# Reordering the work inside an expert tile of a hybrid attention and mixture-of-experts layer: the shares of a result added behind their own down product, the fold ahead of the pick, and a copy of x1 in plain order

## The reference, cut to what matters

```
x1 = x + gt_m * rms_norm(y_mixer, g_post_mix)
h  = rms_norm(x1, g_pre_ffn) * (1 + sc_f) + sh_f
combine = top-1 group, then top-2 experts in it, with gates     # (tokens, 32)
for every expert e:
    a = h @ w1[e];  b = h @ w3[e]                               # "up", 2048 -> 512 twice
    hid = silu(a) * b * combine[:, e]
    y += hid @ w2[e]                                            # "down", 512 -> 2048
out = x1 + gt_f * rms_norm(y, g_post_ffn)
```

## Time and profile before

| | us |
|---|---|
| median of 3 runs | 1523.38 |
| lowest and highest run | 1520.29, 1523.55 |
| the profiled execution | 1522.02 |
| its span, from the first to the last instruction | 1520.2 |

### The profile page before, as it was taken

The page is one execution under the profiler, slowest core; times in us unless marked ns, Lnnn a source line. Parts: engine busy times, 40 slices in busy tenths (PEclk is TensorE's granted clock), DMA queues, the critical chain, the costliest instruction groups (busy, mean ns, idle before and its releaser), DMA issues.

```text
span 1520.2 us, 18000 instructions
## 1 busy us (share of the span) xinstructions
PE 1192.0 (78%) x7075; PEld 537.6 (35%) x7076; DVE 730.6 (48%) x977; ACT 178.1 (12%) x437; POOL 37.0 (2%) x66
## 2 busy tenths in 40 slices
PE   4799999999999998856756765775666579989755
PEld 4688544744444454212212211221221123333211
DVE  5776257777585635522432342243233226655526
ACT  3111132221111120000000000000000001110002
POOL 1001200000000001000000000000000000000000
PEclk9899999999999997978887887888788779999978
DMA  9999977898778778999999999999999999999995
GB/s 354 392 383 384 334 287 311 316 351 323 272 287 348 294 335 342 424 426 424 427 427 424 427 427 426 423 427 428 424 427 426 426 425 429 421 425 427 427 426 204
DMA packets 101636, 581.93 MB, mean 383 GB/s; under 512 B 6648, under 2 KB 31504, under 8 KB 57824
## 3 DMA queue, kind: packets, MB, share of 16 engines
q1 hardware_dynamic: 98000, 571.50, 92.2%
q10 hardware_dynamic: 2384, 7.77, 1.3%
q0 software_dynamic: 1216, 2.17, 0.5%
HBM read 579.29 MB, written 2.13 MB: 382 GB/s over the span
## 4 chain that ended last, share of the span: by engine, by line
PE 52%; DMA 34%; DVE 9%; SPq 2%; issue 1%; ACT 1%; POOL 0%; DVEq 0%; ACTq 0%
DMA stream<-in_w 32%; PE ps L848 12%; PE ps L674 11%; PE ps L759 7%; PE ps L874 6%; PE ps L593 5%; PE ps L804 3%; DMA stream<-in_w_ada 2%; PE ps L810 2%; PE ps L859 2%; SPq L463 2%; PE ps L671 1%; DVE cst L1276 1%; DVE wk L947 1%; DVE stream L1000 1%
## 5 line engine op out<-in xcount | busy, mean ns | idle before, releaser
L848 PE MATMUL ps<-stream,wk 128*32 128x512 f32 x2304 | 310.1, 699 | 251.3 <-DMA stream<-in_w 242.1
L1228 DVE TENSOR_TENSOR acc<-ps,acc 128x2048 f32<-128x2048 f32 x37 | 84.8, 2291 | 554.2 <-PE ps L810 554.2
L848 PEld LDWEIGHTS ps<-stream,wk 128*32 128x32 f32 x2304 | 87.2, 126 | 472.1 <-issue 470.0
L674 PE MATMUL ps<-stream 128*128 128x512 f32 x448 | 197.5, 594 | 0.3 <-PE ps L593 0.3
L874 PE MATMUL ps<-stream,cst 128*32 128x512 f32 x1152 | 131.1, 595 | 14.6 <-DVE cst L1280 14.6
L593 PE MATMUL ps<-stream 128*128 128x256 f32 x512 | 117.7, 393 | 2.2 <-ACT stream L1358 2.2
L674 PEld LDWEIGHTS ps<-stream 128*128 128x128 f32 x448 | 83.3, 190 | 99.2 <-issue 98.5
L759 PE MATMUL ps<-stream 128*128 128x512 f32 x256 | 112.3, 600 | 3.1 <-ACT stream L1462 1.8
L593 PEld LDWEIGHTS ps<-stream 128*128 128x128 f32 x512 | 100.8, 198 | 16.9 <-issue 2.2
L947 DVE SCALAR_TENSOR_TENSOR wk<-stream,cc,wk 128x768 f32<-128x768 f32 (+1 forms) x90 | 83.6, 929 | 11.1 <-DMA stream<-in_w_ada 8.5
L1501 ACT ACTIVATE wk<-ps 128x512 f32<-128x512 f32 x36 | 21.5, 597 | 549.9 <-PE ps L848 549.9
(11 more groups left out here) (258 smaller groups left out, 857.5 us busy)
## 6 DMA issues: line engine op xcount, KB each, us to landing
stream<-in_w SPq DMA_DIRECT2D x192, 2048.0 KB, 34.8
stream<-in_w_ada SPq DMA_DIRECT2D x64, 1024.0 KB, 5.5
stream<-in_w_in SPq DMA_DIRECT2D x8, 4096.0 KB, 16.6
stream<-in_w_ada SPq DMA_DIRECT2D x64, 384.0 KB, 10.0
stream<-in_w_out SPq DMA_DIRECT2D x4, 4096.0 KB, 15.4
stream<-in_w_ada SPq DMA_DIRECT2D x16, 512.0 KB, 9.4
stream<-in_w_in SPq DMA_DIRECT2D x4, 2048.0 KB, 14.3
stream<-in_w_in SPq DMA_DIRECT2D x2, 3072.0 KB, 16.2
```

What stands on the lines that cost most here:

```text
L674: last = nc.tensor.matmul(bank(fill % 2), hT[:, k, P * half:P * half + P], w[:, k, :], start=(k == 0), stop=(k == KD - 1))
L848: last = nc.tensor.matmul(bank(1)[32 * g:32 * g + 32, :], xe[:, k + g // 2, :], a13[g % 2][:, k + g // 2, :], start=(k == 0), stop=(k == K ...
L1228: V.tensor_tensor(y4, ps[:, b0:b0 + 4, :], y4, ALU.add).then_inc(ysum_sb, 1)
```

## The change

On PE a tile now adds the first share of its own result behind its down (with waits for ACT's copy of it, for the spread of this tile and for the earlier `collect`), so that the next tile has only the second share to add behind its up; the fold (L859) stands in front of `pick_rows()`, behind which the wait for `xp` follows at once. On DVE `collect(1, 4)` stands ahead of the chain of the gate, the copy to `xp` behind it, and `collect(0, 4)` at the end of the tile. The wait of the up for `spread` goes. Behind the loop the last tile's first share is already added. POOL, which has nothing to do in the loop, waits for the down of the last tile of expert 30, then copies x1 in plain order into the slot that this frees (`plain(t)`, two copies of 128x2048), and `residual(t)` reads it from there.

```diff
+        def plain(t):
+
+            return stream[:, 4, D * (t + 1):D * (t + 2)]
...
                 with pe.Fori(lo, hi) as t:
                     pe.wait_ge(xe_sb, t + 1)
-                    pe.wait_ge(spread_sb, t + 1)
...
                     pe.wait_ge(ye_sb, t + 1)
+                    pe.wait_ge(spread_sb, t + 1)
                     pe.wait_ge(ysum_sb, 2 * t + 2)
-                    add_part(0, 4)
-                    pe.wait_ge(pick_sb, t + 2)
-                    pick_rows()
+                    add_part(1, 4)
                     pe.wait_ge(ab_sb, t + 1)
                     for c in range(4):
                         last = nc.tensor.matmul(bank(1, 4, RT_W)[:, c, :], ...)
                     last.then_inc(h_ps, 1)
-                    pe.wait_ge(ysum_sb, 2 * t + 3)
-                    add_part(1, 4)
+                    pe.wait_ge(pick_sb, t + 2)
+                    pick_rows()
                     pe.wait_ge(rows_sb, t + 2)
                     pe.wait_ge(gated_sb, t + 1)
...
                     last.then_inc(ye_ps, 1)
+                    pe.wait_ge(spread_sb, t + 2)
+                    pe.wait_ge(ysum_sb, 2 * t + 3)
+                    pe.wait_ge(ye_sb, t + 2)
+                    add_part(0, 4)
...
-            pe.wait_ge(spread_sb, total + 1)
-            pe.wait_ge(ysum_sb, 2 * total + 2)
+            pe.wait_ge(xe_sb, total + 1)
+            pe.wait_ge(ysum_sb, 2 * total + 1)
...
-            earlier_sum(0)
-            pe.wait_ge(ye_sb, total + 1)
-            pe.nop(nofuse=True)
-            add_part(0, 4)
-            for g in range(1, 4):
+            for g in range(4):
                 earlier_sum(g)
             add_part(1, 0, True)
...
                 dve.wait_ge(part_ps, 2 * t + 1)
                 dve.wait_ge(ysum_sb, 2 * t + 2)
-                collect(0, 4)
-                dve.wait_ge(rows_ps, t + 2)
-                V.tensor_copy(xp, bank(0)).then_inc(rows_sb, 1)
-
+                collect(1, 4)
                 dve.wait_ge(h_exp, t + 1)
...
                 V.tensor_tensor(hid, hp[:, :, ROWS:2 * ROWS], eh, ALU.mult).then_inc(hid_sb, 1)
+                dve.wait_ge(rows_ps, t + 2)
+                V.tensor_copy(xp, bank(0)).then_inc(rows_sb, 1)
                 dve.wait_ge(xe_ps, t + 2)
...
                 dve.wait_ge(part_ps, 2 * t + 2)
-                collect(1, 4)
-
-            dve.wait_ge(part_ps, 2 * total + 1)
+                dve.wait_ge(ysum_sb, 2 * t + 3)
+                collect(0, 4)
+
             dve.wait_ge(ysum_sb, 2 * total + 2)
-            dve.nop(nofuse=True)
-            collect(0, 4)
-            dve.wait_ge(ysum_sb, 2 * total + 3)
...
+                dve.wait_ge(plain_sb, t + 1)
                 dve.wait_ge(fin_rs, t + 1)
...
-                    V.scalar_tensor_tensor(out=now, in0=now, scalar=st[:, 80 + t:81 + t], in1=by_model(t)[:, 32 * q:32 * q + 32, :],
+                    V.scalar_tensor_tensor(out=fin_gained(t)[:, c], in0=fin_gained(t)[:, c], scalar=st[:, 80 + t:81 + t], in1=plain(t)[:, c],
...
+            pool.wait_ge(route_sb, 1)
+            done = pool.value_load(cums[0:1, NE - 1:NE], min_val=1, max_val=MAX_TILES)
+            pool.wait_ge(ye_ps, done)
+            pool.nop(nofuse=True)
+            for t in range(TT):
+                nc.gpsimd.tensor_copy(plain(t).rearrange("p (q k) -> p q k", k=KD), by_model(t)).then_inc(plain_sb, 1)
```

More of the change, by code:

```diff
@@ L392, in build @@
             sem("hid_sb"), sem("ye_ps"), sem("ye_sb"))
-        gain_sb, fin_sq, fin_rs, fin_sb, fin_out = sem("gain_sb"), sem("fin_sq"), sem("fin_rs"), sem("fin_sb"), sem("fin_out")
+        plain_sb, gain_sb, fin_sq, fin_rs, fin_sb, fin_out = sem("plain_sb"), sem("gain_sb"), sem("fin_sq"), sem("fin_rs"), sem("fin_sb"), sem("fin_out")
         w_ada = a["w_ada"].rearrange("l (p k) (m n) -> (l p) k m n", p=P, m=6)
@@ L1295, in _ @@
             link(V.tensor_tensor(fin_gained(0), ysum[0], g2b, ALU.mult))
-            dve.wait_ge(part_ps, 2 * total + 2)
+            dve.wait_ge(part_ps, 2 * total + 1)
             dve.nop(nofuse=True)
@@ L1308, in residual @@
                     c = slice(512 * q, 512 * q + 512)
-                    now = fin_gained(t)[:, c].rearrange("p (q k) -> p q k", k=KD)
-                    V.scalar_tensor_tensor(out=now, in0=now, scalar=st[:, 80 + t:81 + t], in1=by_model(t)[:, 32 * q:32 * q + 32, :],
+                    V.scalar_tensor_tensor(out=fin_gained(t)[:, c], in0=fin_gained(t)[:, c], scalar=st[:, 80 + t:81 + t], in1=plain(t)[:, c],
                                            op0=ALU.mult, op1=ALU.add).then_inc(fin_sb, 1)
@@ L1509, in _ @@
             A(st[:, 83:84], cst[:, C_HALF:C_HALF + 1], ACT.Sqrt)
-            act.wait_ge(ysum_sb, 2 * total + 3)
+            act.wait_ge(ysum_sb, 2 * total + 2)
             act.nop(nofuse=True)
```

## The result

The changed kernel takes 1544.9 us (median of 4 runs, 1539.99 to 1545.02) against 1523.47: a ratio of 1.0136, with a 95% interval of 1.0122 to 1.0151. It is slower, as forecast, but by 21.4 us instead of 12, and outside the range. The profiled execution took 1544.78 us and spans 1542.9.

A forecast was written before the change was run, and what follows sets the result against it. From about 600 us the DMA engines' weight transfers were taken as the bound. Transfers +14.7 us and the end -2.7 gave +12.0, from the profiled 1522.02 to 1534.0, as median 1535.4 us; range 1528 to 1541.

The forecast's parts named there:

- where a longer tile is paid: From A's first up to E's second, weight transfers wait for PE; there a longer tile becomes a longer kernel, transfers +14.7 us.
- the two late issues: Weight transfers issued only when the second ups of B and E are done, at 1303.77 and 1391.08 us.
- the sum had 1.2: Slack at the issue behind E's second up: 1.2 us, taken off the 15.9 us by which that up ends later.
- the figure read from the row: Start and landing of transfers behind a late issue: 3.6 us, read from one transfer, against the skill's fixed cost of about 2.0.
- Loss 1: Ahead of the down, PE waits for DVE's copy to `xp`, now behind `hid`: down starts 0.62 us later.
- Loss 2: Behind the down, PE waits for ACT's copy to `ye`, then does `add_part(0, 4)`: +1.80 us a tile.
- The rival by which the wait for `xp` would not be on the path: Tile grows only about 1.0 us, 1524 us in all; needs PE to pass the `xp` wait; chance 0.04.
- The sum over the eight passages: From A's first up to E's second: 8 x 2.42 = 19.4 us, less 3.5 of vanishing waits, so 15.9 later.
- Queued behind this wait on PE is the next up: At the tile's end, the next up stands behind PE's wait for ACT's copy to `ye`; part of +1.80 us.
- a rival of 0.08, all or nothing: TensorE's clock falls in each tile after PE's rests: +15 to +24 us on eight tiles, 1551 to 1559; chance 0.08.
- The end: Last tile and `residual`: 0.34 for `add_part(0, 4)`, 0.2 for the loop exit, -3.26 for faster last sums; -2.7 us.
- falls inside the back-to-back tiles: Sign of a wrong forecast: granted clock dropping in tiles that follow each other without a wait; no size given.

The follow-up runs named there:

- the chain first: Changed kernel with `collect(1, 4)` on DVE moved from ahead of the gate's chain to ahead of `collect(0, 4)`: 1533.08 us, ratio 1.006.
- the part alone: Changed kernel with the pick ahead of the fold again and DVE's copy to `xp` ahead of the gate's chain: 1538.59 us, ratio 1.0094.
- The fold alone: Kernel before with only the fold ahead of the pick and DVE's copy to `xp` behind `hid`; both `add_part` as before: 1526.02 us, ratio 1.0014.
- the copy alone: Kernel before plus GpSimd's two copies of x1 in plain order and the last sums reading them, no reordering: 1520.05 us, ratio 0.9982.

## Why the prediction was wrong, point by point

**What bounds the kernel, and where a longer tile is paid.** Right. The stretch from A's first up to E's second decides, and the two late issues are the ones at which the transfers pause most. The third pause (3.5 us, at the issue behind D's second up) was not forecast; the end does not hang on it, since E's issue is later still (26.6 us). The kernels with intermediate tiles lie between: the issue at E's second up is 14.3, 20.5 and 26.6 us late with the chain first, with the part alone and in the changed kernel, and the last up is 13.0, 18.9 and 24.9 us late. Between 1.3 and 1.7 us were spare, where the sum had 1.2 (a matrix at 425 GB/s takes 9.87 us, not 9.83; with that the sum has 1.5). With the 2.0 us that the Trainium skill gives ("DMA: Bandwidth & Descriptors", section "Anatomy of one DMA") it would have been 2.8, so the figure read from the row was nearer.

**The tile, Loss 1 and Loss 2.** Right in kind and nearly in size: 2.61 us instead of 2.42, which is 1.5 us over eight passages. The fold alone gave 0.53 a tile (forecast 0.62), the part alone 2.10 (forecast 1.80). The rival by which the wait for `xp` would not be on the path falls.

**The sum over the eight passages.** This is the step that failed. "there are eight passages from one tile to the next: 8 x 2.42 = 19.4" counts only what the order of the instructions adds, with PE's sequencer and its clock as they were. Measured, E's second up ended 26.6 us late, not 15.9. The missing 10.7 are:
- 1.5 from the tile's size, above;
- 4.0 from the pauses ahead of B, C, D and E (0.83 + 1.43 + 0.82 + 0.94). The step "Queued behind this wait on PE is the next up" was too short. Also queued there are the reads of the next expert's tile numbers, which the sequencer did ahead of the matmuls before, when nothing held it at the end of a tile. No term or rival had them; the two runs with fewer and more reads show them;
- 5.0 from the clock: 1.7 in A's second down, 1.7 in B's, 1.6 in D's with its transposes. The prediction had this as a rival of 0.08, all or nothing (15 to 24 us). It read correctly that PE would rest 2 us, and took a rest of 1.92 us without a fall as evidence that it would hold. In fact it fell in three of eight tiles.

With these terms the sum is 15.9 + 1.5 + 4.0 + 5.0 = 26.4, against 26.6.

**The end.** -2.24 us instead of -2.7. `add_part(0, 4)` is 0.33 late within the last tile (forecast 0.34), leaving the loop cost nothing (forecast 0.2). The last sums take 747 ns, not 650; together -2.72 instead of -3.26 (the forecast set 8.31 us with one reciprocal against 5.05 with two, which made its gain too small by 0.1 to 0.2). The outputs now come every 0.66 us, and take 3.0 us to land instead of 2.3, which gives 0.6 back; the last up's slow start was 0.4 us shorter. GpSimd's copies took 3.64 us each, within the 2.4 to 5 of the forecast, and were covered.

**The signs.** The sign of being wrong that the clock "falls inside the back-to-back tiles" came true. Of what was to show the forecast right, the transposes waited for the copy to `xp` and this for the product ahead of it, `add_part` stood 0.81 us behind the down (forecast 0.75) and ups 19.34 us apart (19.1); the pauses were larger than "7 to 8 us lost in each" (10.6 and 11.9), the last up started at 1505 instead of 1495, and the last sums took 0.75 us instead of 0.6 to 0.7.

What stays open: which rests are long enough for a fall. In the changed kernel rests of 2.0 us were followed by a fall in three of eight tiles; in the kernel with the part alone, whose rests ahead of the down are 1.2 us, one down was still slow, and so was an up behind rests of 0.81 and 0.90; with rests of 1.0 and 0.8 us no down was. It is not shown why the same rest is followed by a fall in one tile and not in the next, and no run tells what the 1.43 us ahead of C hold beyond the reads (with one read fewer 1.45 remain there, since C is the first of a group of five and its number is read anyway).

## What to carry to other kernels

When an engine's order of work gets a new wait, look at what its sequencer did ahead of time and can't any more: here it was the reading of loop bounds, some 0.65 us each, that had been free as long as matmuls were queued in front of them. And look at PE's rests in the new order: if one grows to the 2.0 us measured here, price a clock that falls in some of the tiles, not in all or none. A change of two parts should be split before it is judged, since here the copy of x1 gains 2.7 us and the reordering loses about 24.

## What was not expected of the hardware

PE's granted clock fell from 2.4 to 1.2 GHz behind rests of 2.0 us, in three of eight tiles, and four idle matmuls (1.7 us) were enough to hold it. Reading a loop bound into a register costs PE some 0.65 us once it is exposed. A read of x1 with 128 float32 elements between neighbours, in `resid`, made DVE's operation 1086 instead of 747 ns for 512 elements; and two GpSimd copies of that pattern took 3.64 us each (3.7 with the copy alone), and DVE operations of 0.16 and 0.29 us took 3.6 and 3.7 us beside them, one of them with 4 elements per partition.
